# A two-layer hybrid diffusion step on one core: the adaLN modulation chunks 8 to 23 formed by VectorE and GpSimd instead of TensorE

## The reference, cut to what matters

```python
mod = (jax.nn.silu(cond) @ w_ada + b_ada)[:, None, :]      # cond: 1 x 1024, w_ada: 1024 x 6144
sh1, sc1, gt1, sh2, sc2, gt2 = jnp.split(mod, 6, axis=-1)
h = rms_norm(x, g_mix) * (1 + sc1) + sh1
p = h @ w_in
...                                                        # three mixers, gates, merge
x = x + gt1 * (merged @ w_out)
h2 = rms_norm(x, g_ffn) * (1 + sc2) + sh2
gu = h2 @ w_ffn_in
x = x + gt2 * ((jax.nn.silu(gu[..., :D_FF]) * gu[..., D_FF:]) @ w_ffn_out)
```

## Time and profile before

| what | value |
|---|---|
| median of three runs | 2227.45 us |
| the profiled execution: its own time, and its span | 2229.23 us, 2227.4 us |
| busy in the span: PE, DVE, ACT, POOL | 1943.7, 1049.3, 837.6, 283.4 us |
| adaLN products (L598), all 48 chunks | 768 records, 181.5 us |
| first layer, start of the projection's products, of attention, GLA, RWKV, and of phase 4 | 85, 220.8, 338, 457, 764 us |

### The profile page before, as it was taken

How to read it: one execution, slowest core, us unless ns; L and a number is a source line. 1 busy time by engine, 2 the same in 40 slices (tenths; PEclk the granted TensorE clock), 3 DMA queues, 4 the chain that set the end, 5 groups by cost and what they waited for, 6 DMA issues and landing times.

```text
span 2227.4 us, 32378 instructions
## 1 busy us (share of the span) xinstructions
PE 1943.7 (87%) x13395; PEld 1549.4 (70%) x13395; DVE 1049.3 (47%) x1931; ACT 837.6 (38%) x1408; POOL 283.4 (13%) x550
## 2 busy tenths in 40 slices
PE   6899998967985798999989989898687668899998
PEld 2799445633554598999979965464354547799998
DVE  0335427754565544343342544384556645543332
ACT  1533534253333535333253345324324334533321
POOL 2000000015555000000000000000553420000000
PEclk9999999978996799999999999999787669999999
DMA  7433333202130143443443423323101003344332
GB/s 256 133 116 105 101 114 123 95 25 76 58 115 20 33 152 95 127 120 108 126 126 111 125 82 114 114 86 100 57 11 48 2 1 109 104 114 133 110 118 85
DMA packets 267768, 214.06 MB, mean 96 GB/s; under 512 B 7209, under 2 KB 259400, under 8 KB 267368
## 3 DMA queue, kind: packets, MB, share of 16 engines
q1 hardware_dynamic: 264640, 204.39, 30.2%
q0 software_dynamic: 2736, 7.54, 1.1%
q10 hardware_dynamic: 248, 0.07, 0.0%
HBM read 209.10 MB, written 2.88 MB: 95 GB/s over the span
## 4 chain that ended last, share of the span: by engine, by line
PE 69%; DVE 11%; ACT 8%; POOL 7%; issue 3%; DMA 1%; DVEq 0%; ACTq 0%; POOLq 0%
PE bank L547 11%; PE bank L549 10%; PE bank L548 10%; PE bank L603 8%; PE bank L598 7%; POOL cst L1129 4%; POOL lora L1127 3%; PE bank L1046 3%; PE bank L1047 3%; PE bank L1048 3%; PE bank L609 3%; PE bank L787 2%; PE bank L499 1%; ACT h L1193 1%; PE bank L713 1%
## 5 line engine op out<-in xcount | busy, mean ns | idle before, releaser
L549 PE MATMUL bank<-scr_rounded 128*128 128x384 f32 (+1 forms) x1312 | 442.3, 337 | 0.0
L603 PE MATMUL bank<-h,ring 128*128 128x384 f32 x640 | 243.9, 529 | 21.9 <-DVEq L337 17.9
L547 PE MATMUL bank<-scr_rounded 128*128 128x384 f32 x672 | 230.5, 343 | 25.7 <-DVE scr_rounded L1606 24.2
L549 PEld LDWEIGHTS bank<-scr_rounded 128*128 128x128 f32 (+1 forms) x1312 | 248.3, 189 | 1.0
L548 PE MATMUL bank<-scr_rounded 128*128 128x384 f32 x672 | 228.1, 339 | 0.0
L1601 DVE TENSOR_TENSOR scr_rounded<-ring,scr_rounded 128x2048 fp32r<-128x2048 f32 (+1 forms) x64 | 136.0, 2126 | 177.9 <-ACT scr_rounded L1184 177.0
L547 PE MATMUL bank<-scr_rounded,gate_rounded 128*128 128x384 f32 (+1 forms) x640 | 214.8, 336 | 4.3 <-DVE scr_rounded L1601 4.3
L548 PE MATMUL bank<-scr_rounded,gate_rounded 128*128 128x384 f32 (+1 forms) x640 | 214.5, 335 | 0.0
L603 PEld LDWEIGHTS bank<-h,ring 128*128 128x128 f32 x640 | 124.7, 204 | 115.0 <-issue 48.6
L598 PE MATMUL bank<-ring,scond 128*2 128x256 f32 x768 | 181.5, 390 | 19.7 <-DVE mg L1591 6.0
L1601 DVE TENSOR_TENSOR scr_rounded<-ring,gate_rounded 128x2048 fp32r<-128x2048 f32 (+3 forms) x64 | 130.1, 2033 | 105.8 <-ACT gate_rounded L1184 105.2
(11 more groups left out here) (357 smaller groups left out, 3238.4 us busy)
## 6 DMA issues: line engine op xcount, KB each, us to landing
ring<-in_w_in_dram SPq DMA_DIRECT2D x56, 1024.0 KB, 5.3
ring<-in_w_ada_dram SPq DMA_DIRECT2D x48, 1024.0 KB, 5.3
ring<-in_w_ffn_in_dram SPq DMA_DIRECT2D x88, 512.0 KB, 5.1
ring<-in_w_ffn_out_dram SPq DMA_DIRECT2D x32, 704.0 KB, 4.6
ring<-in_w_out_dram SPq DMA_DIRECT2D x8, 1024.0 KB, 5.0
ring<-in_w_po_a_dram SPq DMA_DIRECT2D x4, 1024.0 KB, 6.4
ring<-in_w_po_b_dram SPq DMA_DIRECT2D x4, 1024.0 KB, 5.4
ring<-in_w_po_c_dram SPq DMA_DIRECT2D x4, 1024.0 KB, 6.2
```

The costliest lines, as they stand in the source:

```text
L547: pe.matmul(o, w_hi[:, k, :], right[0][k], start=k == 0, stop=False)
L549: ins = pe.matmul(o, w_lo[:, k, :], right[0][k], start=False, stop=k == nk - 1)
L603: ins = pe.matmul(b[:, 0:T], w[:, k, 128 * (j % 2):128 * (j % 2) + 128], h[:, k, :], start=k == 0, stop=k == KD - 1)
```

## The change

Chunks 8 to 23 are formed without TensorE's eight products. VectorE forms for the first condition, on each partition, the sum over the eight row blocks of weight times condition, in eight dependent instructions of 256 columns (`mod_first`). GpSimd then does the same for the second condition in place in the ring slot: one product of 2048 columns and three additions of halves, 1024, 512 and 256 columns (`mod_second`); it starts when VectorE has read the chunk. Both sums lie in `modacc` (which also holds `modrow`, still used for chunks 0 to 7). TensorE then sums over the partitions with four products of a 128 x 128 stationary and one column of ones (`mod_sum`); VectorE adds the bias as before. VectorE's next chunk waits until that product has been made, since `modacc` is there once.

Chunks 8 to 15 are now in the projection phase, and 16 to 23 in attention; GLA has none. `fill(2)` in attention becomes `fill(3)`. The order of the loads follows, and the loads behind an adaLN chunk now wait for `ada_sums`.

```diff
@@ side_plan @@
-                return [("ada", l, 8), ("ada", l, 9)] + [w for j in range(6) for w in (gate_of(0, j), ("ada", l, 10 + j))] + [gate_of(0, 6), gate_of(0, 7)]
+                return [gate_of(0, 0)] + [w for j in range(7) for w in (gate_of(0, j + 1), ("sum", l, 16 + j))] + [("sum", l, 23)]
             if k == 2:
-                ada = [("ada", l, 16 + j) for j in range(8)]
-                po = [po_of(0, j) for j in range(8)]
-                return po[0:4] + ada[0:4] + po[4:8] + [gate_of(1, 0), ada[4], gate_of(1, 1)] + ada[5:8]
+                return [po_of(0, j) for j in range(8)] + [gate_of(1, j) for j in range(2)]
@@ order @@
+            inputs = [(l, "in", j) for j in range(9)] + [(l, "gk", 0)] + [(l, "inc", j) for j in range(8)]
+            for j in range(8):
+                order += inputs[2 * j:2 * j + 2] + [(l, "ada", 8 + j)]
+            order += inputs[16:18]
+            order += [(l, "ada", 16), (l, "gate", 0), (l, "ada", 17), (l, "ada", 18), (l, "gate", 1), (l, "ada", 19), (l, "ada", 20),
+                      (l, "gate", 2), (l, "ada", 21), (l, "ada", 22), (l, "gate", 3), (l, "ada", 23)]
@@ TensorE @@
+            def mod_sum(l, j):
+                count = told("ada_sums", l, j - 7)
+                last_use[order.index((l, "ada", j))] = S["ada_sums"], count
+                pe.wait_ge(S["ada_sums"], count)
+                pe.wait_ge(*fill_room())
+                b = fill_item("V", "sum", l, j)
+                for i in range(2):
+                    for n in range(2):
+                        ins = pe.matmul(b[:, 2 * i + n:2 * i + n + 1], modacc[:, n, 128 * i:128 * i + 128], ones[:, 0:1], start=True, stop=True)
+                ins.then_inc(fill_ready, 1)
@@ projection: after in 1, 3, 5, 7 the sums 8 to 11, after gk sum 12, after inc 1, 3, 5 the sums 13 to 15 @@
+                    if j % 2:
+                        mod_sum(l, 8 + j // 2)
@@ attention, TensorE @@
-                    fill(2)
+                    fill(3)
@@ GpSimd: chunks 8 to 15 before barrier 0, 16 to 23 after the loads of the cache @@
+                def mod_second(j):
+                    w = weights(l, "ada", j)
+                    gp.wait_ge(S["ada_first"], told("ada_first", l, j - 7))
+                    gp.tensor_tensor(w, w, scond[:, 1, :].unsqueeze(2).to_broadcast([128, KD, 256]), mult).then_inc(*step())
+                    gp.wait_ge(*last())
+                    for n in (4, 2):
+                        gp.tensor_tensor(w[:, 0:n, :], w[:, 0:n, :], w[:, n:2 * n, :], add).then_inc(*step())
+                        gp.wait_ge(*last())
+                    gp.tensor_tensor(modacc[:, 1, :], w[:, 0, :], w[:, 1, :], add).then_inc(*tells("ada_sums"))
@@ VectorE @@
+            def mod_first(l, j):
+                w = weights(l, "ada", j)
+                dve.wait_ge(*arrived(l, "ada", j))
+                if j > 8:
+                    side_work("sum", l, j - 1)
+                    dve.wait_ge(fill_ready, filled("sum", l, j - 1))
+                ts(modacc[:, 0, :], w[:, 0, :], scond[:, 0, 0:1], None, mult).then_inc(*step())
+                yield
+                for k in range(1, KD):
+                    dve.wait_ge(*last())
+                    stt(out=modacc[:, 0, :], in0=w[:, k, :], scalar=scond[:, 0, k:k + 1], in1=modacc[:, 0, :], op0=mult, op1=add).then_inc(*(
+                        step() if k < KD - 1 else tells("ada_first")))
+                    yield
@@ VectorE, projection: chunk 8 ahead of split 2, 9 to 13 after splits 3, 5, 7, 9, 11; 14 and 15 after shifts 3 and 7 @@
+                    if m % 2:
+                        for _ in mod_first(l, 8 + m // 2):
+                            pass
@@ VectorE, attention: chunk 16 right after the barrier, then @@
+                mixed = itertools.chain(*(mod_first(l, j) for j in range(17, 24)))
                 for pair in range(NPAIR + 3):
+                    for _ in itertools.islice(mixed, 8 if pair in (4, 9) else 4 if pair < 12 else 0):
+                        pass
```

36 lines of the change are left out of this document (29 added, 7 removed).

## The result

| | time, median | ratio to before, 95% interval |
|---|---|---|
| before | 2229.49 us (median of four, 2226.18 to 2231.72) | |
| after | 2380.11 us (2378.61 to 2387.45) | 1.0688 [1.0665, 1.0710] |

The change costs 151 us. The forecast was +94 (2321 us, range to 2375), so the sign and the kind of mechanism, rings of waits with GpSimd in them, were right and the size too small. All times are medians of three to ten executions; one of e14's ten, at 4559 us, is a slow one and isn't compared.

The account below looks back on a forecast made before the run. The prediction took TensorE to bound the projection, attention and GLA. Projection +28, attention +31 and GLA -12 gave +47 us per layer, +94 for both, so 2321 us for the median; range 2245 to 2375 us.

Parts of the forecast that it names:

- S: TensorE's time for one chunk's sum over the partitions, four fp32 products in eight records: 1.1 us, ends 0.5 and 1.5.
- VectorE's 4.0 us: VectorE's time per chunk for the first condition: one TENSOR_SCALAR and seven dependent instructions of 256 columns, together 4.0 us.
- P: GpSimd's time per chunk for the second condition, product and three additions: 8.4 us, ends 4.7 and 10.
- Rival 1: Same chain but cheaper, P nearer 5 or 6, projection collisions mostly missed: +15 us per layer, 2257 us; chance 0.2.
- rival 2: TensorE counts and GpSimd doesn't close attention's ring, below P = 4.5: -5 us per layer, 2217; chance 0.09 with the rest.
- come at 28, 1 to 2 us before ScalarE wants them; hidden: Projection: loads behind GpSimd's sum, issued at 20 us and landed 8.3 us later, were to cost nothing.
- some 12 us per layer: Blocking at the SBUF port between VectorE's and GpSimd's two-operand instructions: without it the terms would be that much smaller.
- rival 3: Idle time in attention's ring lowers TensorE's clock, gates take twice as long, GLA's saving halves: +73 per layer, 2373; chance 0.13.
- the forecast's waits: Projection: TensorE's waits for late sums, within a total of 27.6 us per layer that includes 1.1 us per sum.
- Attention, +31 forecast: Attention: chunks 17 to 23 form a closed ring of VectorE, GpSimd and TensorE, usually 16.7 us each; +31 us per layer.
- It idles for over 6: Attention: TensorE has about 10 us of work per usual 16.7 us chunk and waits the rest before the sum, seven times.
- GLA, -12 forecast: GLA: rounds lose five adaLN chunks (-8.9 us) and a last chunk leaves the path (3.3 us); -12 us per layer.

Follow-up runs that it names:

- e14: The changed kernel with two copies of the sums, short GpSimd instructions and no gate load in the slot of the gate before: 2228.2 us.
- e5: The changed kernel with the loads of chunks 8 to 15 cut to an eighth: 2366.2 us.
- e12: The changed kernel with the loads of chunks 8 to 15 cut to an eighth and memsets in place of GpSimd's product and additions: 2308.1 us.
- e7: The changed kernel with memsets of about the same total time, which read nothing, in place of GpSimd's product and additions: 2326.2 us.
- e6: The changed kernel with GpSimd's product and first two additions cut to 256 columns: 2274.0 us.
- e1: The changed kernel with chunks 16 to 23 back on TensorE in attention, 8 to 15 left in the projection: 2300.8 us.
- e11: As e4, but VectorE also forms chunks 16 to 18 in attention and GLA keeps five chunks on TensorE: 2166.2 us.
- e4: The changed kernel without GpSimd: VectorE forms both conditions of chunks 8 to 15 in the projection, 16 to 23 on TensorE in GLA: 2185.9 us.

## Why the prediction was too low

- What bounds, what is removed, S, VectorE's 4.0 us and P: right (P 8.2 for 8.4 in attention, 10.2 at sum 11 where the low half collides; S 0.95 for 1.1). Rival 1 (P of 5 or 6) and rival 2 (TensorE binds) fell with P.
- **The failed step** is the last sentence on the projection, that the loads behind GpSimd's sum "come at 28, 1 to 2 us before ScalarE wants them; hidden". I asked when the `in` chunks are wanted, not when VectorE wants the next adaLN chunk, whose load is the first thing issued and whose slot is the one just freed. e5 and e12 measure it: 7.8 us in the first layer, 5 to 12 over both.
- The port was mis-sized: "some 12 us per layer" of the terms. e7 took off 28.5 us (21.2 and 7.3), some 6 of them by its shorter GpSimd, so about 22. I let two operands on both sides collide, and gave attention's normalisations, with one tensor operand, 0.4 us per chunk; single ones took 3.02 us, and a shift 3.65. In the projection GpSimd's additions also stand behind the low half (5.7 for 3.7 us), in the ring.
- A term that the sum has nowhere is TensorE's slower products behind its waits: 13.1 us in the projection and 21 in attention, where they partly fill time in which it would wait anyway. The forecast priced both stretches at the full clock; only rival 3 let gates take longer there, by 3 to 4 us in some cycles. In the projection the forecast's waits (27.6 less eight times 1.1, so 18.8 us) are near TensorE's 20.1 us of added idle time, and the miss of 13 is about the size of the slower products. That the waits agree in sum is luck, since they lie at other sums.
- By the experiments, the projection's +40.8 is 7.6 sums, 7.8 load, 21.2 port and length of GpSimd, and 4.2 left in e12. This and the division by TensorE's time (7.6 sums, 20.1 idle, 13.1 slower) are two accounts of the same 40.8: a wait taken away took its slower products with it, down to a clock of 1.00 in e6.
- Attention, +31 forecast and +42 measured: a ring, with the right period to 7%, but of four engines. The forecast "It idles for over 6" was wrong as to place: the idle time lies in front of gates and transposes, and once in front of a sum. Of the 11 us, about 7 are the steps from sum 16 to 23 (122.0 for 115.3), about 4 the tail (9.8 us for 6, from 410.77 to 420.56), where TensorE's products are slower (3.25 us for the 28 records of L727 that take 1.75 elsewhere).
- Rival 3 came nearest (2373 against 2380), for a partly wrong reason. It wanted P = 9.3, which is not what was measured, so that its number fits is partly luck. Its clock did come: 0.77 in attention's rounds where 1.00 was, and 0.90 in the projection, where it had left it out.
- GLA, -12 forecast and -6.4 measured. The rounds without side work run at VectorE's pace as I said: from the start of the first round's products to the start of the last product of TensorE's outputs (L802 before) 64.2 us instead of 72.2, and from there to RWKV 11.8 instead of 14.9, so -11.1. These two are the same within 0.1 us in every kernel with no adaLN work in GLA. What I missed is ahead of them, 36.9 us for 32.1. In e1, whose attention is as long as before's, it is 38.3 and 35.3, so a slow attention isn't needed for it. The trace of after shows a branch projection of `fill(6)` for 5.46 us at a granted clock of 0.50, VectorE's addition for it in front of its next work, and TensorE waiting for that. That this is the whole of the 4.8 us was not tested.

```profile
440.50 5.46 PE L631 MATMUL bank<-arena,ring 128*128 128x384 f32 x8 [3.00 <-DVE mg L1634]
450.07 1.97 PE L504 MATMUL bank<-cst,scr 128*128 128x128 f32 x8 [4.12 <-DVE scr L1849]
```

- RWKV and phase 4 unchanged: right within 5 us (RWKV 2.5 us longer in the first layer, 4.4 shorter in the second).

The misses per layer are 13 + 11 + 6 = 30 us, 60 for both; the forecast was 59 us short (2380 for 2321).

## What to carry to other kernels

Before giving side work to an idle engine, write down the closed chain of waits for one item of it, with the load of the next item and the slot it goes into, and with whatever stands behind each waiting instruction on each engine; an engine that is "free" has a price as soon as another must wait for it in order. A second chain on the engine that already holds the operands can be cheaper than a first on an idle one (0.40 us an instruction here, 2.2 us a chunk, against 8.2 and a shared port). And a sum that is asked for a round later than it is ready costs only itself. Where waits are added in front of TensorE, price its products behind them at what they take at the lower clock too.

## What the runs showed of the hardware

- Dependent VectorE instructions of 256 columns: 0.515 us each in one chain, 0.40 in two chains taken in turn.
- GpSimd, fp32: 3.60 us for a product of 2048 columns with a broadcast operand (1.76 ns a column), 2.11 ns a column for additions, 1.83 us for a memset of 2048 (0.89 ns).
- GpSimd's memsets leave VectorE's two-operand instructions alone and lengthen its TENSOR_SCALAR of 384 columns from 0.42 to 0.79 us on average; with GpSimd's reads the averages are 1.06 and 1.14, and single ones take up to 3.65.
- Behind a wait of 7.07 us in attention TensorE took 2.93 us for four records that take 1.56 in e11. The granted clock of attention is 0.75 to 0.83 in the kernels with GpSimd's real work there, and 0.98 to 1.00 in e4 and e11.
